# Reordering the last embedding and the last mixer of a two-block transformer kernel: preparation of x ahead of the gates, one square sum in four a unit later, v's last unit by token tiles

## The reference, cut to what matters

```python
def second_block(x, p, ...):
    h = x
    for i in range(DEPTH_2):                                  # 2 layers
        hn = rms_norm_2(h, ln_mix[i])
        if i < N_A_LAYERS: h = h + gdn_mixer(hn, ...)         # layer 0
        else:              h = h + sb_mixer(hn, k_sh, v_sh, ...)   # layer 1: "mixer 3"
        h = h + swiglu_2(rms_norm_2(h, ln_ffn[i]), ...)
        h = h + (p[i] @ ple_w_proj[i]) * jax.nn.sigmoid(rms_norm_2(h, ln_ple[i]) @ ple_w_gate[i])
        if i == N_A_LAYERS - 1:
            k_sh, v_sh = shared_kv(h, kv_norm, w_kv, k_norm)

def shared_kv(h, kv_norm, w_kv, k_norm):
    kv = (rms_norm_2(h, kv_norm) @ w_kv).reshape(b_, s_, 2, SB_HEADS, SB_HEAD_DIM)
    k = rms_norm_2(kv[:, :, 0], k_norm)       # norm over each head's 128
    v = kv[:, :, 1]
```

## Time and profile before

| | |
|---|---|
| time, median of 3 runs | 2512.68 us (2512.59 to 2514.78) |
| the profiled execution: its own time | 2514.78 us |
| its span, first to last instruction | 2514.8 us |
| TensorE busy | 2457.7 us, 98% |
| VectorE busy | 1726.5 us, 69% |
| ScalarE busy | 1252.5 us, 50% |
| GpSimd busy | 1358.7 us, 54% |
| mean granted TensorE clock | 0.996 of full speed |

### The profile page before, as it was taken

One profiled execution on the slowest core, in us unless ns is written; L12 is line 12 of the kernel. 1 busy time (PEld: TensorE's weight loads), 2 busy tenths in 40 slices (PEclk: granted clock), 3 DMA queues, 4 the chain that ended last, 5 costly groups with the idle time before them and its releaser, 6 DMA issues.

```text
span 2514.8 us, 37950 instructions
## 1 busy us (share of the span) xinstructions
PE 2457.7 (98%) x15202; PEld 2108.7 (84%) x15202; DVE 1726.5 (69%) x2551; ACT 1252.5 (50%) x1799; POOL 1358.7 (54%) x672
## 2 busy tenths in 40 slices
PE   8999999999999999999999999999999999999999
PEld 6899987777789999777887889999877777999987
DVE  5777752888677777586666687776687567777755
ACT  5333343568553433567555553333455685343343
POOL 4677754232457777446544357777444224777754
PEclk9999999999999999999999999999999999999999
DMA  4333333111223333222211133333332113333333
GB/s 142 101 101 101 102 113 113 59 59 55 88 89 105 105 102 104 84 76 84 60 35 35 44 100 101 101 101 109 92 92 84 51 34 101 101 101 101 101 102 124
DMA packets 61790, 223.64 MB, mean 89 GB/s; under 512 B 6704, under 2 KB 6832, under 8 KB 61488
## 3 DMA queue, kind: packets, MB, share of 16 engines
q1 hardware_dynamic: 60928, 218.07, 27.5%
q10 hardware_dynamic: 688, 3.15, 0.3%
HBM read 219.10 MB, written 2.10 MB: 88 GB/s over the span
## 4 chain that ended last, share of the span: by engine, by line
PE 78%; DVE 12%; ACT 6%; issue 3%; DMA 1%; POOL 0%; SPq 0%; DVEq 0%; ACTq 0%
PE ps L661 6%; PE ps L662 6%; PE ps L663 6%; PE ps L586 5%; PE ps L588 5%; PE ps L587 5%; PE ps L578 4%; PE ps L577 4%; PE ps L576 4%; PE ps L1799 2%; PE ps L998 2%; PE ps L1800 2%; PE ps L1801 2%; PE ps L1000 2%; PE ps L999 2%
## 5 line engine op out<-in xcount | busy, mean ns | idle before, releaser
L2970 POOL TENSOR_TENSOR w_lo<-raw,w_hi 128x1024 fp32r<-128x1024 f32 (+1 forms) x405 | 942.3, 2337 | 975.5 <-ACT w_hi L496 974.2
L496 ACT ACTIVATE w_hi<-raw 128x1024 fp32r<-128x1024 f32 (+1 forms) x405 | 397.1, 983 | 661.2 <-PE ps L578 432.2
L2977 POOL TENSOR_TENSOR t_lo<-t_sum,t_hi 128x1024 fp32r<-128x1024 f32 x140 | 336.2, 2423 | 50.2 <-DVE t_sum L773 40.9
L661 PE MATMUL ps<-mid_hi,w_hi 128*128 128x512 f32 x704 | 275.4, 391 | 6.6 <-DVE h L887 3.4
L662 PE MATMUL ps<-mid_lo,w_hi 128*128 128x512 f32 x704 | 274.8, 390 | 0.0
L663 PE MATMUL ps<-mid_hi,w_lo 128*128 128x512 f32 x704 | 273.9, 389 | 0.0
L586 PE MATMUL ps<-sx_hi,t_hi 128*128 128x256 f32 x840 | 238.3, 284 | 5.9 <-DVE ff_up L840 5.9
L588 PE MATMUL ps<-sx_hi,t_lo 128*128 128x256 f32 x840 | 238.0, 283 | 0.0
L587 PE MATMUL ps<-sx_lo,t_hi 128*128 128x256 f32 x840 | 238.0, 283 | 0.0
L887 DVE SCALAR_TENSOR_TENSOR h<-ps,h 128x512 f32<-128x512 f32 x320 | 200.5, 683 | 35.3 <-PE ps L663 25.0
L501 ACT ACTIVATE t_hi<-t_sum 128x1024 fp32r<-128x1024 f32 x140 | 148.0, 1061 | 93.3 <-DVE t_sum L771 51.0
(11 more groups left out here) (455 smaller groups left out, 6456.3 us busy)
## 6 DMA issues: line engine op xcount, KB each, us to landing
raw<-in_units_dram SPq DMA_DIRECT2D x406, 512.0 KB, 3.6
h<-in_x_t_dram SPq DMA_DIRECT2D x4, 512.0 KB, 7.1
toep<-in_rel_table_dram ACTq DMA_DIRECT2D x1, 2048.0 KB, 8.0
out_dram<-h SPq DMA_DIRECT2D x4, 512.0 KB, 5.7
p_f<-in_p_t_dram ACTq DMA_DIRECT2D x2, 512.0 KB, 4.8
const<-in_constants_dram SPq DMA_DIRECT2D x1, 832.0 KB, 7.0
vec<-in_vectors_dram SPq DMA_DIRECT2D x1, 137.5 KB, 2.2
```

Source lines behind the costliest of these rows:

```text
L496: nc.scalar.activation(w_hi[:, n % W_SLOTS, begin:], raw[:, n % RAW_SLOTS, begin:], ACT.Copy).then_inc(s_whi, 1)
L661: nc.tensor.matmul(out, hi, mid_hi[:, mid, :], start=(k == 0), stop=False)
L2970: nc.gpsimd.tensor_tensor(w_lo[:, n % W_SLOTS, begin:], raw[:, n % RAW_SLOTS, begin:], w_hi[:, n % W_SLOTS, begin:].bitcast(F32), ALU.subt ...
L2977: nc.gpsimd.tensor_tensor(t_lo[x % 2][part][:, :, :], t_sum[x % 2][part][:, :, :], t_hi[x % 2][:, 2 * part:2 * part + 2, :].bitcast(F32), ...
```

## The change

Three reorderings; no instruction is added, removed or resized.

1. In the embedding, ScalarE prepares tile u-1 ahead of sigmoid u (behind the rounding of a unit of weights), and VectorE prepares tile u-1 ahead of gate product u.
2. In mixer 3, `square_sum(c)` for c = 4, 8, 12 is made after units 7, 11, 15, just ahead of sums 5, 9, 13, and not after units 6, 10, 14.
3. In v's last unit (`kp` = 3) the loop over token tiles m is the outer one and the loop over the two contraction tiles k2 the inner one.

```diff
@@ act_embed
                 if u:
                     act_ahead(act, n0, 0, u)
+                    if gain is not None:
+                        act_prep(act, w, [u - 1], gain, lambda m: act.wait_ge(s_hup, w.hups + m + 1), x_hi=mid_hi)
                 act.wait_ge(s_free, b0 + u + 5)
                 nc.scalar.activation(ff_gate[:, u % 2, :], ff_gate[:, u % 2, :], ACT.Sigmoid).then_inc(s_gact, 1)
-                if gain is not None:
-                    if u:
-                        act_prep(act, w, [u - 1], gain, lambda m: act.wait_ge(s_hup, w.hups + m + 1), x_hi=mid_hi)
@@ dve_embed
             for u in range(8):
+                if gain is not None and u:
+                    dve_prep(dve, w, [u - 1], gain, x_hi=mid_hi, x_lo=mid_lo)
                 dve.wait_ge(s_used, n0 + u + 1)
...
                 nc.vector.tensor_tensor(h[:, u, :], h[:, u, :], ff_gate[:, u % 2, :], ALU.add).then_inc(s_hup, 1)
-                if gain is not None and u:
-                    dve_prep(dve, w, [u - 1], gain, x_hi=mid_hi, x_lo=mid_lo)
@@ pe_mixer3
-                if u >= 2:
+                if u >= 2 and u not in (6, 10, 14):
+                    if u in (7, 11, 15):
+                        square_sum(u - 3)
                     square_sum(u - 2)
...
-                for k2 in range(2):
+                items = [(k2, m) for k2 in range(2) for m in range(NB)]
+                if kp == 3:
+                    items = [(k2, m) for m in range(NB) for k2 in range(2)]
+                for k2, m in items:
                     k = 2 * kp + k2
```

More of the change, by code:

```diff
@@ L2578, in pe_mixer3 @@
                 pe.wait_ge(s_wlo, unit + 1)
-                for k2 in range(2):
+                items = [(k2, m) for k2 in range(2) for m in range(NB)]
+                if kp == 3:
+                    items = [(k2, m) for m in range(NB) for k2 in range(2)]
+                for k2, m in items:
                     k = 2 * kp + k2
                     hi, lo = w_hi[:, slot, k2 * T:(k2 + 1) * T], w_lo[:, slot, k2 * T:(k2 + 1) * T]
[L2582 to L2591, removed]
+                    if k == 0:
+                        pe.wait_ge(s_free, b0 + 17 + m)
+                    t_hi, t_lo = mid_hi[:, k, m * P:(m + 1) * P], mid_lo[:, k, m * P:(m + 1) * P]
+                    out = ps[:, m, :]
+                    nc.tensor.matmul(out, t_hi, hi, start=(k == 0), stop=False)
+                    nc.tensor.matmul(out, t_lo, hi, start=False, stop=False)
+                    last = nc.tensor.matmul(out, t_hi, lo, start=False, stop=(k == DK - 1))
+                    if k == DK - 1 and m < 3:
+                        last.then_inc(s_bank, 1)
                 last.then_inc(s_used, 1)
```

## The result

Measured in alternation, five runs each: 2522.51 us after (2521.67 to 2524.60), 2514.78 us before (2512.59 to 2516.79). The ratio is 1.0035 [1.0024, 1.0046]. The forecast was 2520.4 in a range of 2513.5 to 2524.5, and slower by more than 0.2% with a chance of 0.74.

A forecast was written before the change was run, and what follows sets the result against it. The prediction took the embedding to be bound by its VectorE and ScalarE loop, not TensorE. Loss 6.2 + clock 1.5 + 0 + 0 = 7.7 us, on the 2512.7 us median 2520.4 us, range 2513.5 to 2524.5.

The forecast's parts named there:

- Period, 6.14 us: Embedding loop: sigmoid to next sigmoid takes 6.14 us, as POOL's subtraction delays mid_lo; TensorE needs 5.5 us a unit.
- The one place of the old trace with the new order: Embedding at u = 0, w_hi right behind a sigmoid: w_lo ends 3.72 us after that sigmoid.
- the literal reading: Embedding: mid_lo runs its full 0.74 us after POOL, not 0.55; 1.3 us more in seven units, 2521.7 us.
- Part one, 6.2 us: Embedding: the last mid_lo ends at 1862.14, before at 1855.96, so TensorE's eighth tile and norm sum start 6.2 us later.
- Clock, 1.5 us: Behind the eighth tile: TensorE's two pauses drop the clock to 1.2 GHz; net cost 1.5 us, bounds 0 and 3.5.
- The forecast's two terms: Clock drop behind the eighth tile: 2.0 us lost over some 4 us, some 0.5 back at the first n_lo wait.
- The rival without a drop: Embedding loop late, but the clock stays at 2.4 GHz: 2518.9 us, chance 0.22.
- one pause of 3.45 us: TensorE at 68.98 in the old trace: a pause by itself, ending in a matmul of 0.50; evidence against a drop.
- Part two, 0: Mixer 3's square sums 4, 8, 12: sum 5 still starts when n_lo ends; 0, bounds 1.4 us gain, 0.3 loss.
- Part three, 0: v's last unit: last eviction ends when it did, mask copies stand behind it; 0, bounds 0 and 0.1 us.
- The sum, 7.7 us: Whole kernel: 6.2 + 1.5 + 0 + 0 = 7.7 us; 2522.5 on the profiled execution, 2520.4 against the median.
- No rival: Rivals: POOL not in the way 0.12; all three stalls go 0.04; late loop, clock up 0.22; collisions in some units 0.10.

The follow-up runs named there:

- short_lo_new: The changed kernel with GpSimd's subtraction cut to 64 of 1024 columns in the seven units beside the embedding; 2512.80 us, 0.9995 of before.
- filled_pauses: The changed kernel with 13 and 16 unused matmuls put into TensorE's two pauses at the seventh and eighth tile; 2519.98 us, 1.0024 of before.
- gates_alone: The kernel before with only the embedding's reordering (preparation ahead of the gates), square sums and v unchanged; 2523.97 us, 1.0035 of before.
- round_behind: The changed kernel with ScalarE's rounding of weights moved behind the preparation in the embedding; 2520.66 us, 1.0028 of before.
- sixth_sum: The kernel before with square sums 5, 9 and 13 made one unit later, 4, 8 and 12 unmoved; 2511.48 us, 0.9991 of before.
- short_lo_old: The kernel before with GpSimd's subtraction cut to 64 of 1024 columns in the seven units beside the embedding; 2512.24 us, 0.9997 of before.
- two_moves: The kernel before with square sums 5, 9, 13 one unit later, mask copies ahead of v's evictions, v's last unit by token tiles; 2509.92 us, 0.9985 of before.
- last_round_late: The kernel before with the rounding of weights in the embedding's last unit moved behind the last preparation; 2514.50 us, 1.0003 of before.
- masks_early: The kernel before with the two mask copies moved ahead of v's evictions in VectorE's order; 2513.59 us, 0.9998 of before.

## Why the prediction was right, step by step

**Period, 6.14 us.** Measured 6.13 from mid_lo to mid_lo. Sigmoid to end of w_lo: 3.71 for 3.72 (1821.35 to 1825.06). Rest of mid_lo: 0.56 for 0.55. The one place of the old trace with the new order was enough. The Trainium skill's page "SBUF — State Buffer", section "Who interferes with whom", is right here on who blocks whom, and short_lo_new agrees: with the subtraction cut short, mid_lo is back at 0.75. (The runs show who holds up whom; that what the two share is a port, no run here shows.) But the rest behind the subtraction is 0.54 to 0.56 us in two different instructions, not the full 0.69 to 0.75 they take alone. The prediction's sum by the literal reading, 2521.7, lies nearer to the 2522.51 than the forecast, but not because of that term: the median of before moved.

**Part one, 6.2 us.** mid_lo 7 ends at 1861.08 after and at 1855.96 before, by the anchors 50.04 and 43.98: 6.06 us. Pauses of 3.3 and 4.1 were forecast; from start to start, less 0.23, they are 3.26 and 4.06 (1856.28 less 1852.79, and 1861.13 less 1856.84).

**Clock, 1.5 us.** A drop was forecast and came (granted clock 0.50), and filled_pauses prices it at 1.28 to 1.36 us. From the table: 7.57 at sum 0 less 6.06 leaves 1.51; filled_pauses, with the clock up, still loses 6.21 there, 0.15 more than 6.06, of which 0.09 is its own mid_lo 7, which ends 50.13 behind its anchor. The forecast's two terms were 2.0 us lost and 0.5 given back. The first seven matmuls from the eighth tile on take 4.00 us after (1861.13 to 1865.13) and 2.12 before, 1.88 lost:

```profile
1858.14 0.40 PE L2562 MATMUL ps<-mid_hi,w_lo 128*128 128x512 f32 x1
```

(before, counted from 1856.02). The gap ahead of sum 0 is 0.33 us after (1875.34 to 1875.67) and was 0.66 (1868.38 to 1869.04), so 0.33 came back. The rival without a drop had 2518.9; the kernel without a drop measures 2519.98.

The ground on which the chance of a drop was set is weaker than it looked. The prediction set one pause of 3.45 us that left the clock up against a pair of pauses that did not. But that single pause (3.4 to 4.0 us in the fourteen traces), in a layer that all kernels here have alike, left it up only in before: in each of the other thirteen traces a half-clock stretch begins within 2 us of its end. After has it so, with the granted clock at 0.50 from 68 to 72:

```profile
67.23 0.79 PE L661 MATMUL ps<-mid_hi,w_hi 128*128 128x512 f32 x1 [3.44 <-DVE h L887]
```

These traces, of which the prediction knew one, make the drop likelier than it was put, and that it takes two pauses is not shown. At the seam it came in all three kernels with long pauses there: after, gates_alone and round_behind.

**Part two, 0.** n_lo in front of sum 5 is late whatever is ahead of it. TensorE after:

```profile
1905.77 0.39 PE L2544 MATMUL ps<-n_hi,ones_r 128*128 128x512 f32 x1
1906.00 0.39 PE L2545 MATMUL ps<-n_lo,ones_r 128*128 128x512 f32 x1
1907.05 0.50 PE L2544 MATMUL ps<-n_hi,ones_r 128*128 128x512 f32 x1 [0.66 <-DVE n_lo L2832]
```

Sum 4 now runs just ahead of sum 5, and the gap is the same 1.05 us as in the earlier trace rows. sixth_sum shows the other half of the argument: moving the sum that waits does gain.

**Part three, 0.** VectorE after:

```profile
1979.61 0.75 DVE L2856 TENSOR_SCALAR v<-ps,rcol 128x512 f32<-128x512 f32 x1 [0.61 <-PE ps L2592]
1980.41 0.22 DVE L2859 CAST tri_r<-const 128x128 fp32r<-128x128 f32 x1
```

Each eviction now waits for its token tile, the last one starts 0.43 us behind TensorE's last matmul (1979.18), where it was about 0.5, and the copies stand behind it. From that matmul to the first scores it is 1.50 us, and was 1.51. What the prediction did not say is that the copies hide a gain of part three: without them it is worth 0.4 to 0.5 us.

**The sum, 7.7 us** on the profiled execution: 7.44 by the anchors. Against the medians it is 2522.51 less 2514.78 = 7.73, with an interval of about 6.0 to 11.6 us by the ratio, so that the close fit rests on the traces. The forecast in absolute terms, 2520.4, is 2.1 us low because it stood on a median of 2512.7 from three runs; the five runs of before taken with after have 2514.78. No rival came true. One expectation of the experiments fell outright: for short_lo_old a larger part of the old seam stall was expected to stay than did. With the subtraction out of the way the embedding's old loop keeps up with TensorE, whose list has no wait for mid_lo there, and at sum 0 it is only 0.3 us behind the new one, where 0.7 was expected. Others missed in size only: sixth_sum gained 2.97 us up to the scores for 2.5 to 2.8, and two_moves 4.17 in all for 4.5.

The end of short_lo_old gains only 0.51 us where its scores gained 1.20. The rest goes in a half-clock stretch that this trace alone has there, at 2068 us. It makes one group of nine matmuls 0.9 us longer than in before (short_lo_old, its window, then before):

```profile
2067.38 2.45 PE L2650 MATMUL ps<-sb_lo,tri_r 128*128 128x512 f32 x9 [0.34 <-DVE sb_lo L2888]
...
2068.00:2070.00 2.00, 2.00 (x9) 1.91 (x9) 0.13 (x1) 0.63 (x1) 2.00 (x2) 0.50 0.00 0
...
2073.08 1.56 PE L2650 MATMUL ps<-sb_lo,tri_r 128*128 128x512 f32 x9 [0.35 <-DVE sb_lo L2888]
```

By the anchors this group still starts 1.21 us sooner than in before; the next that waits for VectorE, 0.45. What stays open is why the clock fell there, and why parts of the same program run at half clock in one trace and not in the next.

## What to carry to other kernels

Before moving an instruction on one engine, ask what its end releases, and what the released engine shares: here ScalarE's rounding released GpSimd's subtraction, and that held VectorE up just as the loop came round to it, in all seven turns. Moving the work ahead of a stall gains nothing if what the stall waits for does not move; move the one that waits, or take away the work that stands ahead of what it waits for. A step that measures nothing can still be worth something behind another one, as part three is behind the mask copies.

## What the runs showed of the hardware that was not expected

- VectorE's instruction under a GpSimd subtraction ends 0.54 to 0.56 us behind it whether it is mid_lo (0.75 alone) or the gate product (0.69 alone). The gate's first product, with one input from PSUM, shows no such wait: in before all eight take 0.677 to 0.691 us, and four of them lie inside a subtraction, the last at 1850.41 in one that runs from 1849.94 to 1852.77.
- Two pauses of TensorE of 3.1 and 3.9 us of idle time with three matmuls between them brought the clock to 0.50; filled with work nobody uses, the same places leave it at 1.00. One and the same pause of 3.4 to 4.0 us in an earlier layer left the clock up in one trace of fourteen.
- Ahead of the seam all fourteen kernels are the same program, and yet stretches at half clock come and go there: before has them at 19.6, 98 and 1057 us, after at 66, 377 and 1056, each some 3 to 10 us long. The event from which the table counts lies between 1805.76 us (last_round_late) and 1812.52 (filled_pauses). The stretches alone do not make this spread: masks_early and last_round_late have the same two, near 67 and 1056 us, and are 2.59 us apart at that event. Differences of a few us are therefore better read from one event to another within the trace than from two times.
